# Strassen–Winograd feed-forward: the second group's first product moved ahead of the first group's summed products, and the down projection begun with its three products without sums

## The chip, the cores and the metric

The kernel runs on one core of a Trainium2 chip. TensorE (PE) multiplies, VectorE (DVE) and ScalarE (ACT) do the work on elements, GpSimd (POOL) has little to do here, SyncE (SP) issues the loads of weights. The metric is the device time of one execution in microseconds (us); of several runs the median counts.

## The reference, cut to what matters

The network is two blocks one after the other on 256 tokens of width 1024, all in float32. The parts that the change touches are its feed-forwards, six in all:

```python
def conv_ffn(h, norm_g, w_up, conv_w, conv_b, w_down):          # twice, in the first block
    u = dwconv_centred(rmsnorm(h, norm_g) @ w_up, conv_w, conv_b)
    return (jax.nn.gelu(u[..., :D_FF]) * u[..., D_FF:]) @ w_down

def swiglu(h, wg, wu, wd):
    return (jax.nn.silu(h @ wg) * (h @ wu)) @ wd

def half_ffn(h, g, shift, scale, gate, wg, wu, wd):              # four times, in the second block
    return h + 0.5 * gate * swiglu(modulate(rms_norm(h, g), shift, scale), wg, wu, wd)
```

`D_FF` is 2816, which is 22 tiles of 128 (`FT`); 1024 is 8 tiles (`KT`). The first three half feed-forwards work on 512 columns (256 tokens of context and 256 of the latent), the last one and the two convolutional ones on 256.

## The kernel before

**Seven products in place of eight.** The feed-forward is done in groups of two output tiles by two halves of the columns. A group is a 2 by 2 block product, and class `Fast` computes it with seven products in place of eight, as Winograd's form of Strassen's method does. Call them P1 to P7, as `q` in the code. P1 and P2 use the weights and the activations as they are. P3 uses the weights' last sum and plain activations. P4 uses plain weights and the activations' last sum. P5, P6 and P7 use a sum of weights and a sum of activations each. One product is 4 tiles deep in the up projection (gate and up together) and 11 deep in the down projection, and each depth step of float32 shows as two records in the profile, so that a product has 8 or 22 of them. A product is 256 columns wide ("wide") in the first three half feed-forwards and 128 ("narrow") in the last one and in the convolutional ones.

**The groups.** `i` counts them: 0 to 21 are the gate/up groups, one for each tile of the hidden layer, and 22 to 25 are the four groups of the down projection, each of two output tiles. The convolutional feed-forwards compute their up projection in another way and use `Fast` for groups 22 to 25 alone. P5(22) stands below for the fifth product of group 22.

**The order on TensorE** is that in which `tensor_fast` writes it. It goes through the groups and in each through `PRODUCTS`, which is P1, P5, P6, P7, P3, P2, P4; in group 0 of a half feed-forward it is `FIRST_PRODUCTS`, which is P1, P3, P2, P5, P6, P7, P4, since the activation sums are not there yet. TensorE takes its instructions in that order, and each wait stands in front of a product. P1 and P2 add up in `bank_a`, P7 and P4 in `bank_c`. For that reason P2 waits until P1 has been copied out (by ScalarE, line 1537, in group 0 line 1523), and P4 waits until P7 has been read (by VectorE, line 1617). P1 of the next group waits for the silu that reads `bank_a` (line 1545), or, in the down projection, for the addition to x that reads it (line 1589 or, with the gate of a half feed-forward, 1591, called by line 1645).

**VectorE** takes its instructions in the order of `vector_fast`. For each group it adds u = P1 + P6 (1610), reads P7 (1617), reads P5 twice (1619, 1621) and P3 (1624). In the down projection it then adds two of the four results to x (1639, 1641), makes two weight sums of the next group (1643), adds the third result, which stands in `bank_a`, to x (1645), makes a third weight sum, reads P4 (1653), adds the fourth result and makes the fourth sum. A weight sum (line 1570) is 128 x 512 in the up projection and 128 x 1408 in the down one. The activation sums are made once for a projection, in `vector_activation_sums`: T1 (line 1575) for P5, T2 for P6, one in place for P7, T4 for P4. In the down projection they are as large as half of the hidden layer.

**The loads** of down weights go into a ring of four slots. The load of a later group waits for P2 and P4 of the group whose slots it takes.

Of the kernel before, what the change touches and what calls it, by code (L numbers as in the profile page):

```python
# [11 lines left out]
ACT = mybir.ActivationFunctionType  # L12
# [15 lines left out]
FT = D_FF // 128  # L28
# [70 lines left out]
def build(nc, ins, out):  # L99
# [1253 lines left out]
    bank_a, bank_b, bank_c, bank_d, bank_e = acc[0], acc[1], acc[2], acc[3], aux[0]  # L1353
# [54 lines left out]
    class Fast:  # L1408
# [3 lines left out]
        def __init__(self, t0, up=True, hid_at=None, rows=None):  # L1412
# [11 lines left out]
            for i in range(self.start, n):  # L1424
                for q in FIRST_PRODUCTS if i == 0 else PRODUCTS:
                    if (i < FT and q == 4 and i % 2) or (i >= FT and q in PRODUCTS[-2:]):
                        self.done[i, q] = (acc_full, next(ends))
                    else:
                        self.done[i, q] = (st_p, st_p.reserve(1)(0))
# [39 lines left out]
    def tensor_fast(F, norm_ready=None, following=None):  # L1469
        for i in range(F.start, F.n):  # L1470
            up, j, first = i < FT, i - F.start, i == F.start
            for blk in F.blocks_of(i):
                te.wait_ge(weights_in[blk.slot].sem, blk.arrived_at)
# [6 lines left out]
            banks = {1: bank_a, 2: bank_a, 3: bank_e, 4: bank_c, 5: bank_d, 6: bank_b, 7: bank_c}  # L1480
            for q in FIRST_PRODUCTS if i == 0 else PRODUCTS:
                if q in SUM_FOR:
                    te.wait_ge(st_s.sem, F.s(4 * j + (SUMS if i else FIRST_SUMS)[SUM_FOR[q]]))
                if q in TERM_FOR and i in (F.start, FT):
                    te.wait_ge(st_t.sem, F.t((4 if j and i == FT else 0) + TERM_FOR[q]))
                if q == 1 and first and not up:
                    for b in range(4):
                        te.wait_ge(acc_free[b].sem, F.banks[b])
                elif q == 1 and not first and i <= FT:
                    te.wait_ge(st_g1.sem, F.g1(i - 1))  # L1490
                elif q == 1 and not first:
                    te.wait_ge(st_x.sem, F.x(4 * (i - FT - 1) + 2))
                elif q == 2:
                    te.wait_ge(st_u.sem, F.u(j))
                elif q == 3 and not first:
                    te.wait_ge(st_c12.sem, F.c12(j - 1))
                elif q == 4:
                    te.wait_ge(st_v.sem, F.v(j))
                elif q == 5 and not first:
                    te.wait_ge(st_d.sem, F.d(j - 1))  # L1500
                elif q == 6 and not first:
                    te.wait_ge(st_b.sem, F.b(j - 1))
                elif q == 7 and not first:
                    te.wait_ge(st_c21.sem, F.c21(j - 1))
                lhs, rhs = operands[q]
                for k in range(kt):
                    if i == 0 and q in (1, 3, 2):
                        sig, value = norm_ready(k if q == 1 else 4 + k, 1 if q == 3 else 0)
                        te.wait_ge(sig.sem, value)
                    elif i == FT and q == 1:  # L1510
                        sig, value = (st_hid, F.hid(2 * k + 1)) if F.up else F.hid_at(k)
                        te.wait_ge(sig.sem, value)
                    ins_ = mm(banks[q][:, 0:F.H], lhs[:, k, :], rhs[:, k, :], k == 0 and q not in (2, 4), k == kt - 1)
                F.done[i, q][0].on(ins_)
        if following is not None:
            tensor_norm(following)
        else:
            te.wait_ge(st_x.sem, F.x(14))
            te.wait_ge(st_c21.sem, F.c21(F.n - 1 - F.start))

    def scalar_first_copy(F):
        ac.wait_ge(F.done[0, 1][0].sem, F.done[0, 1][1])
        st_u.on(ac.copy(F.temps[0][:, 0, :], bank_a[:, 0:F.H]))

    def scalar_fast(F, following=None):
        u, v, g1, g2 = F.temps
        for i in range(F.start, F.n):
# [3 lines left out]
            if i:  # L1531
                ac.wait_ge(F.done[i, 1][0].sem, F.done[i, 1][1])
                if j >= 2 and i - 2 < FT:
                    ac.wait_ge(st_hid.sem, F.hid(2 * (i - 2) + 1))
                elif j >= 2:
                    ac.wait_ge(st_x.sem, F.x(4 * (i - 2 - FT) + 3))
                st_u.on(ac.copy(u[:, s, :], bank_a[:, 0:F.H]))  # L1537
# [3 lines left out]
            if i < FT:  # L1541
# [3 lines left out]
                st_g1.on(ac.activation(g1[:, s, :], bank_a[:, 0:F.H], ACT.Silu))  # L1545
# [38 lines left out]
    def vector_fast(F, gate_of=None, following=None):  # L1584
# [8 lines left out]
        for i in range(F.start, F.n):  # L1593
# [43 lines left out]
            if down >= 0:  # L1637
# [7 lines left out]
                add_back(2 * down, 0, bank_a[:, 0:F.H])  # L1645
# [1412 lines left out]
```

## Time and profile before

| | |
|---|---|
| median of 3 runs | 2951.45 us (2949.49 to 2951.77) |
| the profiled execution | 2949.65 us, of it 2948.3 us of span |
| granted TensorE clock, mean | 0.997 of full speed |
| PE busy | 2858.4 us, 97% of the span |
| DVE busy | 1702.3 us, 58% |
| ACT busy | 602.3 us, 20% |
| DMA | 376.15 MB, mean 128 GB/s |

PE is busy in nearly the whole span. What is left to find are short gaps between its products. The timelines further down show them: each line is a run of instructions of one engine on one tile, and the brackets at its end tell how long the engine stood idle before it and which instruction released it.

### The profile page before, as it was taken

How to read it: one execution, taken by the hardware profiler on the slowest of the kernel's cores; microseconds unless marked ns; L12 is line 12 of the kernel's file. 1: busy time of each engine (PE TensorE's matmuls, PEld its weight loads, DVE VectorE, ACT ScalarE, POOL GpSimd, SP SyncE). 2: the span in 40 equal slices, each digit the busy share in tenths (PEclk: the TensorE clock that was granted, in tenths of full speed). 3: DMA queues.
4: the chain of work that ended last, by engine and by line, in shares of the span. 5: the costliest groups of instructions: out<-in, count | busy, mean ns of one | idle time of the engine just before them, and what ended most of it. 6: DMA issues, size and time to landing. Idle time of an engine off the chain costs nothing.

```text
span 2948.3 us, 41101 instructions
## 1 busy us (share of the span) xinstructions
PE 2858.4 (97%) x16754; PEld 2351.4 (80%) x16754; DVE 1702.3 (58%) x3407; ACT 602.3 (20%) x1371; POOL 37.6 (1%) x60
## 2 busy tenths in 40 slices
PE   8988999999999999999999999999999999999999
PEld 7777888977889888888644468888888888766999
DVE  4386467444566477773225457775377773235775
ACT  1264221134221310000124420000110100234110
POOL 0000000020000000000000000000000000000000
PEclk9999999999999999999999999999999999999999
DMA  6400475562665545423213034432444423322444
GB/s 239 139 2 3 167 237 149 189 170 95 218 227 135 186 145 171 152 70 113 75 31 114 3 127 162 160 115 75 133 142 157 152 85 92 106 79 86 144 145 113
DMA packets 349215, 376.15 MB, mean 128 GB/s; under 512 B 7299, under 2 KB 302612, under 8 KB 348260
## 3 DMA queue, kind: packets, MB, share of 16 engines
q1 hardware_dynamic: 323748, 285.68, 31.6%
q10 hardware_dynamic: 23072, 82.52, 7.6%
q0 software_dynamic: 2208, 5.31, 0.9%
q8 instruction: 135, 2.21, 0.3%
q14 instruction: 52, 0.43, 0.0%
HBM read 372.44 MB, written 1.05 MB: 127 GB/s over the span
## 4 chain that ended last, share of the span: by engine, by line
PE 91%; DVE 4%; ACT 3%; issue 1%; DMA 0%; SPq 0%; DVEq 0%; ACTq 0%
PE acc L134 76%; PE aux L134 14%; ACT sb_xn L302 1%; PE aux L2558 1%; DVE sb_work L1570 1%; DVE sb_big L1400 0%; DMA sb_work<-c_decay 0%; DVE sb_work L1400 0%; PE aux L2020 0%; ACT sb_rstd L290 0%; DMA sb_x<-xT 0%; DVE sb_xn L278 0%; DVE sb_work L2769 0%; ACT sb_rstd L292 0%; ACT sb_work L2666 0%
## 5 line engine op out<-in xcount | busy, mean ns | idle before, releaser
L134 PE MATMUL acc<-sb_xn,weights 128*128 128x256 f32 (+3 forms) x5184 | 1218.9, 389 | 17.9 <-DVE sb_xn L278 8.2
L134 PEld LDWEIGHTS acc<-sb_xn,weights 128*128 128x128 f32 (+1 forms) x5184 | 942.0, 190 | 246.8 <-issue 122.9
L134 PE MATMUL acc<-sb_work 128*128 128x256 f32 (+1 forms) x1944 | 374.1, 346 | 2.9 <-DVE sb_work L1575 2.9
L134 PEld LDWEIGHTS acc<-sb_work 128*128 128x128 f32 x1944 | 323.6, 191 | 38.2 <-issue 4.0
L134 PE MATMUL acc<-sb_work,weights 128*128 128x256 f32 (+2 forms) x1508 | 322.2, 361 | 5.8 <-DVE sb_work L1617 3.5
L134 PE MATMUL acc<-sb_big,weights 128*128 128x256 f32 (+1 forms) x1776 | 315.5, 334 | 4.1 <-issue 3.9
L134 PEld LDWEIGHTS acc<-sb_big,weights 128*128 128x128 f32 x1776 | 279.7, 192 | 31.0 <-issue 5.5
L134 PEld LDWEIGHTS acc<-sb_work,weights 128*128 128x128 f32 x1508 | 254.1, 191 | 54.3 <-issue 26.4
L1537 ACT COPY sb_work<-acc 128x256 f32<-128x256 f32 (+1 forms) x108 | 36.7, 340 | 683.9 <-PE acc L134 683.9
L1610 DVE TENSOR_TENSOR sb_work<-sb_work,acc 128x256 f32<-128x256 f32 (+1 forms) x112 | 42.6, 381 | 218.0 <-PE acc L134 218.0
L1543 ACT ACTIVATE sb_work<-sb_work 128x256 f32<-128x256 f32 (+1 forms) x88 | 34.4, 391 | 562.3 <-DVE sb_work L1624 562.3
L134 PE MATMUL aux<-sb_xn,sb_work 128*128 128x256 f32 (+1 forms) x704 | 148.6, 354 | 0.1
L1570 DVE TENSOR_TENSOR sb_work<-weights 128x512 f32<-128x512 f32 (+1 forms) x112 | 99.7, 890 | 75.0 <-PE acc L134 73.6
L134 PEld LDWEIGHTS aux<-sb_xn,sb_work 128*128 128x128 f32 x704 | 122.0, 190 | 14.2 <-ACT sb_xn L302 0.3
L1400 DVE SCALAR_TENSOR_TENSOR sb_work<-sb_work 128x1024 f32<-128x1024 f32 x100 | 122.1, 1221 | 1.4
L1400 DVE SCALAR_TENSOR_TENSOR sb_big<-sb_work 128x1024 f32<-128x1024 f32 x100 | 121.9, 1219 | 0.0
L134 PE MATMUL aux<-sb_big,sb_work 128*128 128x128 f32 (+3 forms) x592 | 109.3, 339 | 0.0
L1624 DVE TENSOR_TENSOR sb_work<-sb_work,aux 128x256 f32<-128x256 f32 (+1 forms) x112 | 42.5, 379 | 103.5 <-PE aux L134 103.5
L1570 DVE TENSOR_TENSOR weights<-weights 128x512 f32<-128x512 f32 (+1 forms) x112 | 99.6, 890 | 2.9
L1570 DVE TENSOR_TENSOR sb_work<-sb_work,weights 128x512 f32<-128x512 f32 (+1 forms) x112 | 99.3, 886 | 3.0 <-DVE sb_work L1570 0.5
L1570 DVE TENSOR_TENSOR sb_work<-weights,sb_work 128x512 f32<-128x512 f32 (+1 forms) x112 | 99.2, 885 | 0.7
L134 PEld LDWEIGHTS aux<-sb_big,sb_work 128*128 128x128 f32 (+1 forms) x592 | 88.7, 185 | 10.9 <-issue 2.8
(352 smaller groups left out, 2664.5 us busy)
## 6 DMA issues: line engine op xcount, KB each, us to landing
weights<-ffn_w_up SPq DMA_DIRECT2D x88, 1024.0 KB, 9.1
weights<-ffn_w_down SPq DMA_DIRECT2D x48, 1408.0 KB, 7.1
sb_work<-w_mod_rows ACTq DMA_DIRECT2D x100, 512.0 KB, 6.0
weights<-ffn_w_gate SPq DMA_DIRECT2D x44, 1024.0 KB, 5.5
sb_big<-w_mod_rows ACTq DMA_DIRECT2D x44, 512.0 KB, 4.8
weights<-mix_w_in SPq DMA_DIRECT2D x5, 2048.0 KB, 12.6
weights<-ple_w_gate SPq DMA_DIRECT2D x4, 2048.0 KB, 7.9
weights<-na_w_qkv SPq DMA_DIRECT2D x8, 1024.0 KB, 7.9
```

Source lines behind the costliest of these rows:

```text
L134: return te.matmul(o, lhsT, rhs, start=start, stop=stop, skip_group_check=True)
L302: shifted.on(ac.activation(y, y, ACT.Identity, bias=N.shift(k, h)))
L1400: rows_done.on(ve.scalar_tensor_tensor(row if s else R.junk, row, 1.0, R.silu_cond[:, s, :], ALU.mult, ALU.mult, accum_out=mod[:, R.first ...
L1537: st_u.on(ac.copy(u[:, s, :], bank_a[:, 0:F.H]))
L1543: st_g2.on(ac.activation(g2[:, s, :], g2[:, s, :], ACT.Silu))
L1570: st_s.on(ve.tensor_tensor(to, one, other, op))
L1610: st_b.on(ve.tensor_tensor(u, u, bank_b[:, 0:F.H], ALU.add))
L1624: st_c12.on(ve.tensor_tensor(g2, g2, bank_e[:, 0:F.H], ALU.add))
L2558: ins_ = te.transpose(aux[u % 3][:, c:c + 128], mx_e[:, u % 4, W * i + 128 * kt:W * i + 128 * kt + 128], ident[:])
```

## The change

Three things are changed in `Fast`, all in the order of TensorE and in the bank of one group.

1. In the half feed-forwards P1 of group 1 is moved from behind P4(0) to in front of P5(0). It goes to a bank of its own: `bank_a` of group 1 is `aux[2]`, and of all other groups `acc[0]` as before. Its wait for the silu of group 0 is left out.
2. In the first down group (22) of all six feed-forwards the order is P1, P3, P2, P5, P6, P7, P4 in place of P1, P5, P6, P7, P3, P2, P4.
3. P3(22) and P2(22) now wait at each of their depth steps for the hidden tile that they read, as P1(22) did before.

The orders of VectorE, ScalarE, GpSimd and SyncE stay as they are.

```diff
-    PRODUCTS, FIRST_PRODUCTS = (1, 5, 6, 7, 3, 2, 4), (1, 3, 2, 5, 6, 7, 4)
+    PRODUCTS = (1, 5, 6, 7, 3, 2, 4)
+    FIRST_TWO = [(0, 1), (0, 3), (0, 2), (1, 1)] + [(0, q) for q in (5, 6, 7, 4)] + [(1, q) for q in (5, 6, 7, 3, 2, 4)]
...
-    bank_a, bank_b, bank_c, bank_d, bank_e = acc[0], acc[1], acc[2], acc[3], aux[0]
+    bank_b, bank_c, bank_d, bank_e = acc[1], acc[2], acc[3], aux[0]
+
+    def bank_a(i):
+        return aux[2] if i == 1 else acc[0]
...
-            for i in range(self.start, n):
-                for q in FIRST_PRODUCTS if i == 0 else PRODUCTS:
...
+            self.order = [(i, q) for i in range(self.start, n) for q in PRODUCTS]
+            if up:
+                self.order[0:2 * len(PRODUCTS)] = FIRST_TWO
+            at = len(PRODUCTS) * (FT - self.start)
+            self.order[at:at + len(PRODUCTS)] = [(FT, q) for q in (1, 3, 2, 5, 6, 7, 4)]
...
-        for i in range(F.start, F.n):
+        for i, q in F.order:
...
-                elif q == 1 and not first and i <= FT:
-                    te.wait_ge(st_g1.sem, F.g1(i - 1))
-                elif q == 1 and not first:
+            elif q == 1 and not first and i != 1 and i <= FT:
+                te.wait_ge(st_g1.sem, F.g1(i - 1))
+            elif q == 1 and not first and i != 1:
...
-                    elif i == FT and q == 1:
-                        sig, value = (st_hid, F.hid(2 * k + 1)) if F.up else F.hid_at(k)
+                elif i == FT and q in (1, 3, 2):
+                    f = k if q == 1 else FH + k
+                    sig, value = (st_hid, F.hid(2 * f + 1)) if F.up else F.hid_at(f)
```

The place in the up projection is seen on TensorE at the start of the first half feed-forward. Before, the rows from P5(0) to P5(1) (acc3 is the bank of P5, acc1 that of P6, acc2 that of P7 and P4, acc0 that of P1 and P2) are:

```order
L134 MATMUL acc3<-sb_work 128x256 [waits activation_sum_set,weight_sum_set]
L134 MATMUL acc3<-sb_work 128x256 x3
L134 MATMUL acc1<-sb_work 128x256 [waits activation_sum_set,weight_sum_set]
L134 MATMUL acc1<-sb_work 128x256 x3
L134 MATMUL acc2<-sb_xn,weights2 128x256 [waits activation_sum_set,weight_sum_set]
L134 MATMUL acc2<-sb_xn,weights2 128x256 x3
L134 MATMUL acc2<-sb_work,weights2 128x256 [waits seventh_product_read,activation_sum_set]
L134 MATMUL acc2<-sb_work,weights2 128x256 x3
L134 MATMUL acc0<-sb_xn,weights2 128x256 [waits left_gate_set]
L134 MATMUL acc0<-sb_xn,weights2 128x256 x3
L134 MATMUL acc3<-sb_work 128x256 [waits fifth_product_read,weight_sum_set]
```

After the change the same stretch reads:

```order
L134 MATMUL aux2<-sb_xn,weights2 128x256 x4
L134 MATMUL acc3<-sb_work 128x256 [waits activation_sum_set,weight_sum_set]
L134 MATMUL acc3<-sb_work 128x256 x3
L134 MATMUL acc1<-sb_work 128x256 [waits activation_sum_set,weight_sum_set]
L134 MATMUL acc1<-sb_work 128x256 x3
L134 MATMUL acc2<-sb_xn,weights2 128x256 [waits activation_sum_set,weight_sum_set]
L134 MATMUL acc2<-sb_xn,weights2 128x256 x3
L134 MATMUL acc2<-sb_work,weights2 128x256 [waits seventh_product_read,activation_sum_set]
L134 MATMUL acc2<-sb_work,weights2 128x256 x3
L134 MATMUL acc3<-sb_work 128x256 [waits fifth_product_read,weight_sum_set]
```

P1(1) has gone from between P4(0) and P5(1) to the head of the stretch, and P5(1) now follows P4(0) directly.

The place in the down projection is seen on TensorE in group 22 of the first convolutional feed-forward (aux0 is the bank of P3). Before, the rows from P5(22) to P4(22) are:

```order
L134 MATMUL acc3<-sb_xn,sb_work 128x128 [waits activation_sum_set,weight_sum_set]
L134 MATMUL acc3<-sb_xn,sb_work 128x128 x10
L134 MATMUL acc1<-sb_work 128x128 [waits activation_sum_set,weight_sum_set]
L134 MATMUL acc1<-sb_work 128x128 x10
L134 MATMUL acc2<-sb_big,weights2 128x128 [waits activation_sum_set,weight_sum_set]
L134 MATMUL acc2<-sb_big,weights2 128x128 x10
L134 MATMUL aux0<-sb_big,sb_work 128x128 [waits weight_sum_set]
L134 MATMUL aux0<-sb_big,sb_work 128x128 x10
L134 MATMUL acc0<-sb_big,weights1 128x128 [waits first_product_copied]
L134 MATMUL acc0<-sb_big,weights1 128x128 x10
L134 MATMUL acc2<-sb_work,weights2 128x128 [waits seventh_product_read,activation_sum_set]
```

After the change the same stretch, with the beginning of P1(23) as its last row, reads:

```order
L134 MATMUL aux0<-sb_big,sb_work 128x128 [waits hidden_tile_set] x10
L134 MATMUL acc0<-sb_big,weights1 128x128 [waits hidden_tile_set,first_product_copied]
L134 MATMUL acc0<-sb_big,weights1 128x128 [waits hidden_tile_set] x10
L134 MATMUL acc3<-sb_xn,sb_work 128x128 [waits activation_sum_set,weight_sum_set]
L134 MATMUL acc3<-sb_xn,sb_work 128x128 x10
L134 MATMUL acc1<-sb_work 128x128 [waits activation_sum_set,weight_sum_set]
L134 MATMUL acc1<-sb_work 128x128 x10
L134 MATMUL acc2<-sb_big,weights2 128x128 [waits activation_sum_set,weight_sum_set]
L134 MATMUL acc2<-sb_big,weights2 128x128 x10
L134 MATMUL acc2<-sb_work,weights2 128x128 [waits seventh_product_read,activation_sum_set]
L134 MATMUL acc2<-sb_work,weights2 128x128 x10
L134 MATMUL acc0<-sb_big,weights3 128x128 [waits x_half_added,weights_arrived0,weights_arrived3]
```

P3 and P2, which stood between P7(22) and P4(22), have moved in front of P5(22). P4(22) with its wait `seventh_product_read` now follows P7(22) directly, and P1(23) with its wait `x_half_added` comes one product after P7(22) in place of three.

## Rows read from the trace of the kernel before

**Rows 1.** The page, part 4: the chain that ended last, by engine.
```profile
PE 91%; DVE 4%; ACT 3%; issue 1%; DMA 0%; SPq 0%; DVEq 0%; ACTq 0%
```

**Rows 2.** Waits of PE, whole run: us in total, times, longest us.
```profile
PE acc L134 <- DVE sb_xn L1575: 2.5, 2, 2.0
```

**Rows 3.** Timeline, first half feed-forward, groups 0 and 1: start us, us, engine.
```profile
1030.58 1.99 PE L134 MATMUL acc<-sb_xn,weights 128*128 128x256 f32 x8 [0.86 <-ACT sb_work L1523]
...
1033.54 3.69 PE L134 MATMUL acc<-sb_work 128*128 128x256 f32 x16 [0.96 <-DVE sb_work L1575]
...
1039.07 0.42 DVE L1617 TENSOR_TENSOR sb_work<-sb_work,acc 128x256 f32<-128x256 f32 x1 [1.08 <-PE acc L134]
...
1039.63 1.97 PE L134 MATMUL acc<-sb_work,weights 128*128 128x256 f32 x8 [0.67 <-DVE sb_work L1617]
...
1040.40 0.68 DVE L1570 TENSOR_TENSOR sb_work<-weights 128x512 f32<-128x512 f32 x1
...
1043.16 3.62 PE L134 MATMUL acc<-sb_work 128*128 128x256 f32 x16
```

**Rows 4.** Timeline, fourth (narrow) half feed-forward, groups 0 and 1.
```profile
2738.47 1.95 PE L134 MATMUL acc<-sb_work 128*128 128x128 f32 x16
...
2740.26 1.06 PE L134 MATMUL acc<-sb_xn,weights 128*128 128x128 f32 x8
...
2741.42 0.29 DVE L1617 TENSOR_TENSOR sb_work<-sb_work,acc 128x128 f32<-128x128 f32 x1 [0.61 <-PE acc L134]
...
2742.02 0.28 DVE L1624 TENSOR_TENSOR sb_work<-sb_work,aux 128x128 f32<-128x128 f32 x1
...
2745.14 0.28 DVE L1653 TENSOR_TENSOR sb_work<-sb_work,acc 128x128 f32<-128x128 f32 x1
...
2745.64 1.06 PE L134 MATMUL acc<-sb_xn,weights 128*128 128x128 f32 x8
```

**Rows 5.** Timeline, first half feed-forward, group 22, P1 to P1(23).
```profile
1296.76 4.91 PE L134 MATMUL acc<-sb_big,weights 128*128 128x256 f32 x22
...
1301.50 4.91 PE L134 MATMUL acc<-sb_xn,sb_work 128*128 128x256 f32 x22
...
1320.77 0.42 DVE L1624 TENSOR_TENSOR sb_work<-sb_work,aux 128x256 f32<-128x256 f32 x1 [3.67 <-PE aux L134]
...
1325.45 0.48 DVE L1591 SCALAR_TENSOR_TENSOR sb_x<-acc,sb_small,sb_x 128x256 f32<-128x256 f32 x1
...
1329.99 0.38 PE L134 MATMUL acc<-sb_big,weights 128*128 128x256 f32 x1
```

**Rows 6.** Timeline, first convolutional feed-forward, group 22, P1 to P1(23).
```profile
489.06 4.32 PE L134 MATMUL acc<-sb_big,weights 128*128 128x128 f32 x22 [1.95 <-issue]
...
493.80 2.69 PE L134 MATMUL acc<-sb_xn,sb_work 128*128 128x128 f32 x22 [0.42 <-DVE sb_xn L1575]
...
503.97 0.29 DVE L1624 TENSOR_TENSOR sb_work<-sb_work,aux 128x128 f32<-128x128 f32 x1 [1.77 <-PE aux L134]
...
507.97 0.28 DVE L1589 TENSOR_TENSOR sb_x<-acc,sb_x 128x128 f32<-128x128 f32 x1
...
508.62 2.62 PE L134 MATMUL acc<-sb_big,weights 128*128 128x128 f32 x22
```

**Rows 7.** Timeline, second convolutional feed-forward, group 22: P1, P5 and P1(23).
```profile
907.40 2.69 PE L134 MATMUL acc<-sb_big,weights 128*128 128x128 f32 x22 [1.96 <-issue]
...
912.14 4.32 PE L134 MATMUL acc<-sb_xn,sb_work 128*128 128x128 f32 x22 [2.05 <-DVE sb_xn L1575]
...
928.74 2.69 PE L134 MATMUL acc<-sb_big,weights 128*128 128x128 f32 x22
```

**Rows 8.** Timeline, fourth half feed-forward: last addition from bank_a, then P1(23).
```profile
2893.48 0.34 DVE L1591 SCALAR_TENSOR_TENSOR sb_x<-acc,sb_small,sb_x 128x128 f32<-128x128 f32 x1
...
2894.00 2.66 PE L134 MATMUL acc<-sb_big,weights 128*128 128x128 f32 x22
```

**Rows 9.** Windows: stretch, its us, PE, PEld, DVE, ACT, POOL busy, PEclk, DMA share, GB/s.
```profile
490.00:491.00 1.00, 1.00 (x7) 1.00 (x6) 1.00 (x2) 0.00 (x0) 0.00 (x0) 0.50 1.16 342
```

More of the change, by code:

```diff
@@ L1423, in __init__ @@
             self.done = {}
-            for i in range(self.start, n):
-                for q in FIRST_PRODUCTS if i == 0 else PRODUCTS:
[L1426 to L1429, printed above, removed]
+            self.order = [(i, q) for i in range(self.start, n) for q in PRODUCTS]
[3 more added lines that the diff above has]
+            self.order[at:at + len(PRODUCTS)] = [(FT, q) for q in (1, 3, 2, 5, 6, 7, 4)]
+            for i, q in self.order:
+                if (i < FT and q == 4 and i % 2) or (i >= FT and q in PRODUCTS[-2:]):
+                    self.done[i, q] = (acc_full, next(ends))
+                else:
+                    self.done[i, q] = (st_p, st_p.reserve(1)(0))
             m = n - self.start
@@ new lines, in tensor_fast @@
+            banks = {1: bank_a(i), 2: bank_a(i), 3: bank_e, 4: bank_c, 5: bank_d, 6: bank_b, 7: bank_c}
+            if q in SUM_FOR:
+                te.wait_ge(st_s.sem, F.s(4 * j + (SUMS if i else FIRST_SUMS)[SUM_FOR[q]]))
+            if q in TERM_FOR and i in (F.start, FT):
+                te.wait_ge(st_t.sem, F.t((4 if j and i == FT else 0) + TERM_FOR[q]))
+            if q == 1 and first and not up:
+                for b in range(4):
+                    te.wait_ge(acc_free[b].sem, F.banks[b])
+            elif q == 1 and not first and i != 1 and i <= FT:
+                te.wait_ge(st_g1.sem, F.g1(i - 1))
+            elif q == 1 and not first and i != 1:
+                te.wait_ge(st_x.sem, F.x(4 * (i - FT - 1) + 2))
+            elif q == 2:
+                te.wait_ge(st_u.sem, F.u(j))
+            elif q == 3 and not first:
+                te.wait_ge(st_c12.sem, F.c12(j - 1))
+            elif q == 4:
+                te.wait_ge(st_v.sem, F.v(j))
+            elif q == 5 and not first:
+                te.wait_ge(st_d.sem, F.d(j - 1))
+            elif q == 6 and not first:
+                te.wait_ge(st_b.sem, F.b(j - 1))
+            elif q == 7 and not first:
+                te.wait_ge(st_c21.sem, F.c21(j - 1))
@@ new lines, in tensor_fast @@
+            lhs, rhs = operands[q]
+            for k in range(kt):
+                if i == 0 and q in (1, 3, 2):
+                    sig, value = norm_ready(k if q == 1 else 4 + k, 1 if q == 3 else 0)
+                    te.wait_ge(sig.sem, value)
+                elif i == FT and q in (1, 3, 2):
+                    f = k if q == 1 else FH + k
+                    sig, value = (st_hid, F.hid(2 * f + 1)) if F.up else F.hid_at(f)
+                    te.wait_ge(sig.sem, value)
+                ins_ = mm(banks[q][:, 0:F.H], lhs[:, k, :], rhs[:, k, :], k == 0 and q not in (2, 4), k == kt - 1)
@@ L1515, in tensor_fast @@
+            F.done[i, q][0].on(ins_)
         if following is not None:
@@ L1522, in scalar_first_copy @@
         ac.wait_ge(F.done[0, 1][0].sem, F.done[0, 1][1])
-        st_u.on(ac.copy(F.temps[0][:, 0, :], bank_a[:, 0:F.H]))
+        st_u.on(ac.copy(F.temps[0][:, 0, :], bank_a(0)[:, 0:F.H]))
     def scalar_fast(F, following=None):
@@ L1536, in scalar_fast @@
                     ac.wait_ge(st_x.sem, F.x(4 * (i - 2 - FT) + 3))
-                st_u.on(ac.copy(u[:, s, :], bank_a[:, 0:F.H]))
+                st_u.on(ac.copy(u[:, s, :], bank_a(i)[:, 0:F.H]))
             if F.rows and 2 <= i <= ROWS_UNTIL:
@@ L1544, in scalar_fast @@
                 ac.wait_ge(F.done[i, 2][0].sem, F.done[i, 2][1])
-                st_g1.on(ac.activation(g1[:, s, :], bank_a[:, 0:F.H], ACT.Silu))
+                st_g1.on(ac.activation(g1[:, s, :], bank_a(i)[:, 0:F.H], ACT.Silu))
                 if F.rows and i == 0:
@@ L1644, in vector_fast @@
                 ve.wait_ge(F.done[i, 2][0].sem, F.done[i, 2][1])
-                add_back(2 * down, 0, bank_a[:, 0:F.H])
+                add_back(2 * down, 0, bank_a(i)[:, 0:F.H])
                 if late:
```

35 lines of the change are left out of this document (3 added, 32 removed).

## The prediction

> **What bounds the kernel now.** I read the chain of waits first: PE holds 91% of it [rows 1], so that only what PE does or waits for counts. PE's list of waits then tells what the change can take away. Its wait for T1 in the down projection comes to 2.5 us in two places [rows 2]. Its wait for T1 at the start of the up projection is 0.96 us at the first half feed-forward [rows 3]; the second and third, which are as wide, repeat this place to within 0.01 us, and the fourth has none [rows 4]. That is all that the new orders can hide: some 5.5 us, and what a gap does to the clock. Last I read the timelines of PE and DVE around each place where the order changes, to see which waits stood behind cover that now moves. In PE's rows the time from the start of one product to the start of the next is what counts; it comes to 1.73 us for a wide up product (the 16 records at 1043.16 are two of them) and 0.89 for a narrow one (two from 2738.47 to 2740.26) [rows 3, 4], to 4.75 for a wide down product (six from 1301.50 to 1329.99) and 2.47 for a narrow one (six from 493.80 to 508.62) [rows 5, 6]. I call E the moment at which the next product could follow P7 with no wait.
>
> **Part 1, the up projection, wide (three times).** P2(0) starts at 1030.58 and with its 0.08 us of restart would be followed at 1032.38; P5(0) starts at 1033.54 [rows 3]. P1(1) with its 1.73 us now fills that gap of 1.16 us, and P5(0) starts at 1034.11. Two products and P7(0) later E comes 0.49 us later than before. P4(0) still waits for L1617, which begins 0.28 us behind E, lasts 0.42 and is seen by PE 0.14 later (1039.07 to 1039.63 [rows 3]), so it starts at 1040.12. It is now followed by P5(1), not by P1(1): 1043.16 - 1.73 + 0.49 = 1041.92, which is **1.24 us earlier**. Is something late instead? P5(1) needs the first weight sum of group 1, which DVE begins 1.33 us behind L1617 and which lasts 0.68 [rows 3]: ready at 1041.7, 0.2 us before it is wanted. The copy of P1(1), now out of aux2, comes behind the silus as before and has a product and a half to spare. So 3 x -1.24 = **-3.7**.
>
> **Part 1, narrow (once).** Here P5(0) did not wait [rows 4]. P1(1) in front of it just makes P5(0), P7(0) and L1617 0.89 us later, and with L1617 all that DVE does up to L1653, which reads P4(0): it ran at 2745.14 and now at 2746.03. P7(1) waits for it, and 0.28 + 0.14 us later is 2746.45. By PE's own order P7(1) would be at 2745.64 as before [rows 4]. P1(1) was the cover of DVE's four weight sums, and it is gone: **+0.8**, and since DVE's row of work stays 0.89 late to P4(1), I take **+0.85**.
>
> **Part 2, the gap at P5(22).** P1, P3, P2 now run while DVE makes T1, and P3's weight sum and the last hidden tile are there before P1(22) ends. The gain is the gap: none in the three wide ones, where P5(22) follows P1(22) at 4.74 us [rows 5] (the whole run has only the two waits of rows 2), none in the fourth half feed-forward (under 0.1), 0.58 us in the first convolutional one (489.06 + 4.32 - 0.16 to 493.80 [rows 6]; 0.16 is how far the modelled end of a product overlaps the next) and 2.27 in the second (907.40 + 2.47 to 912.14 [rows 7]).
>
> **Part 2, what P3 and P2 covered.** They stood between P7(22) and P4(22) and hid two things. (a) P4(22) waits for L1617: E + 0.28 + 0.42 + 0.14 = E + 0.84 wide (as at P4(0) [rows 3]), E + 0.27 + 0.29 + 0.14 = E + 0.70 narrow [rows 4]. (b) P1(23) waits for the addition that reads bank_a, and in DVE's order two weight sums of 1408 columns and two other additions stand ahead of it, all behind the reads of P7, P5 and P3. From L1617 to L1624 it is 0.60 narrow [rows 4], 1.00 wide (0.33 for each of three). From L1624 to that addition it is 4.00 narrow (503.97 to 507.97 [rows 6]) and 4.68 wide (1320.77 to 1325.45 [rows 5]); the wide one may have stood for the end of P2 for some of it, and I take 4.6. Then the addition, 0.48 wide and 0.28 narrow, and 0.14. So P1(23) can start at E + 0.28 + 1.00 + 4.6 + 0.48 + 0.14 = **E + 6.5 wide** and at E + 0.27 + 0.60 + 4.00 + 0.28 + 0.14 = **E + 5.29 narrow**, while P4(22) would be through at E + 5.6 and E + 3.2. Before, this work lay under P2 and P4: narrow, PE reached P1(23) just when it was free.
>
> Place by place, P1(23) after against before:
> - wide, three times: E = 1296.76 + 6 x 4.75 = 1325.26, P1(23) at 1331.76 against 1329.99 [rows 5]: +1.77, in all **+5.3**;
> - first convolutional: E = 493.22 + 5 x 2.47 = 505.57, P1(23) at 510.86 against 508.62 [rows 6]: **+2.2**;
> - fourth half feed-forward: before, P4 was followed at 2894.00 with no wait, so E = 2894.00 - 2.47; its additions are about 0.06 us longer each (0.34 against 0.28 [rows 6, 8]), which makes E + 5.47: **+3.0**;
> - second convolutional: E = 907.40 + 6 x 2.47 = 922.22, P1(23) at 927.51 against 928.74 [rows 7]: -1.2 if its slow stretch goes, **+0.5** if an equal one stays.
>
> **The clock.** In two places 22 records took 4.32 us in place of 2.69 [rows 6, 7], 1.63 us more. The granted clock there is 0.50 [rows 9], that is 1.2 GHz; before each, PE had stood idle for 1.95 and 2.05 us. A third idle time of 1.96 us, at 907.40, was followed by no such stretch [rows 7]. After the change five idle times of about 2 us stand in the kernel: the two before P1(22) of the convolutional feed-forwards, and a new one before P1(23) in each of the three narrow down projections (E + 3.17 to E + 5.29, 2.1 us). The wide ones leave 0.9 us, too short by these rows. Two of three had the drop before; about half of five is 2 to 3 after. I take between none and one stretch more than in the profiled run: +0 to +1.6.
>
> The section "Why this matters for your kernels" of the Trainium skill's page "TensorE: Matmul & The Clock Gate" lets only longer idle gaps than these lower the clock; by it no gap here, old or new, costs a stretch. The rows speak against it (1.95 us idle, then 0.50). By it the sum would stay at +8.15 with no upper case.
>
> **The sum**, against the profiled execution's own 2949.65 us: -3.7 + 0.85 + 5.3 + 2.2 + 3.0 + 0.5 = **+8.15**, with as many slow stretches as it had. That gives 2957.8, and one stretch more 2959.4. The median of the runs is 1.8 us above the profiled one, as much as one such stretch, and from it the two are 2959.6 and 2961.2. I predict **2960**.
>
> The other edits at nothing: the 22 more waits for hidden tiles in P3(22) and P2(22) stand for tiles that are there (P1(22) has such waits and its 22 records take 2.69 us [rows 7], as those of P5(22) without them [rows 6]). Down weights of group 24 may be issued two to three products earlier, since P2(22) ends earlier; nobody waited for them.
>
> **Rivals.**
> - *The DVE row is not late* (the other side: not slower). If the additions that free bank_a were done by the time P4(22) is through, only (a) is paid: wide +0.84 each, first convolutional +0.1, fourth half +0.7, second convolutional -1.6 with its stretch kept. Sum: -3.7 + 0.85 + 2.5 + 0.1 + 0.7 - 1.6 = -1.2, or -2.8 without the stretch: 2947 to 2950. It decides from DVE needing under 5.6 us wide and 3.2 us narrow from E to the addition's end; the rows say 6.4 and 5.2. Chance 0.07.
> - *The clock falls in all the new idle times*: +8.15 and two to three stretches, 2961 to 2965.5. Chance 0.12.
> - *The clock is kept*: the second convolutional's stretch is gone and the new idle times bring none, +4.9 to +6.5: 2954.5 to 2958. Chance 0.14.
> - *The up projection's gain is given back* where DVE, late with its sums in groups 1 and 20, bounds it anyway: +8.15 + 3.7, 2961.5 to 2963.5. Against it, DVE's late work waits for PE's products and so moves with them. Chance 0.05.
> - The forecast, 2957.5 to 2961.5: 0.62.
>
> **The numbers.** The range takes in the kept clock and nearly all of the drops: 2955 to 2965. A measurement here can tell 0.2%, 5.9 us, from no change, so slower begins at 2957.4. Slower holds the forecast without its low edge (0.57), the two dear rivals (0.17) and a part of the kept clock (0.04): 0.78. Same holds the rest of those and most of the first rival: 0.19. Faster: 0.03.
>
> **What would show it.** Right: in PE's waits, L1575 gone for sb_xn and for the wide up starts; new waits of 0.5 to 0.7 us for the read of P7 at six P4(22); new waits at six P1(23) for the addition to x, 0.7 to 0.9 us wide and 2.0 to 2.2 narrow; a new wait of some 0.8 us at P7(1) of the fourth half feed-forward. P1(22) to P1(23) of the first half feed-forward grows from 33.2 to 35.0 us. Wrong: if P1(23) follows P4(22) with no gap, or if gaps of 2 us at P1(23) show 0.50 clock nowhere or everywhere.

## The result, and the profile after

The changed kernel took 2964.99 us, median of 4 runs (2963.09 to 2967.69), beside 2950.59 us of the kernel before in 4 runs. The ratio is 1.0045 with a 95% interval of 1.0033 to 1.0057: **slower by about 13 us** (the medians lie 14.4 us apart). It was timed twice more, beside many more runs of the kernel before, and came to 1.0034 (1.0022 to 1.0046) and 1.0037 (1.0023 to 1.0050), which is 10 to 11 us. Over 68 runs in the batches of the experiments the kernel before spreads from 2949.1 to 2958.2 us; the four runs of it in the first comparison are all at the low end, and that comparison shows some 3 us more than the others.

I read PE's list of waits first. These are lines of it that changed, in the profiled execution of the changed kernel. Lines past the diff have moved by ten: 1627 was 1617 (the read of P7), 1663 was 1653 (the read of P4), 1580 was 1570 (the weight sums), and 1599 and 1601 are the additions to x. The numbers are us in total, times, longest us.

```profile
PE acc L134 <- DVE sb_work L1627: 7.2, 11, 1.0
...
PE acc L134 <- DVE sb_work L1663: 5.1, 5, 1.6
PE acc L134 <- DVE sb_x L1599: 4.1, 2, 2.2
PE acc L134 <- DVE sb_x L1601: 3.8, 4, 2.1
```

The waits for T1 are gone, all five, those of [rows 2] among them. In their place PE waits for the read of P7 in 11 places where it was 5, and in six places for an addition to x, which PE did not wait for before. Those six are the P1(23) of the six feed-forwards.

The timeline of PE at the first down group of the first half feed-forward answers to [rows 5]. In the brackets stand the idle time before the line and what ended it.

```profile
1306.48 4.91 PE L134 MATMUL acc<-sb_big,weights 128*128 128x256 f32 x22
1311.23 4.91 PE L134 MATMUL aux<-sb_big,sb_work 128*128 128x256 f32 x22
...
1330.22 4.91 PE L134 MATMUL acc<-sb_big,weights 128*128 128x256 f32 x22
1335.81 4.99 PE L134 MATMUL acc<-sb_work,weights 128*128 128x256 f32 x22 [0.67 <-DVE sb_work L1627]
1341.38 4.99 PE L134 MATMUL acc<-sb_big,weights 128*128 128x256 f32 x22 [0.58 <-DVE sb_x L1601]
```

P1(22) starts at 1306.48 and P1(23) at 1341.38: 34.90 us where it was 33.23. What held P1(23) is seen in DVE's timeline of the same stretch:

```profile
1335.24 0.42 DVE L1627 TENSOR_TENSOR sb_work<-sb_work,acc 128x256 f32<-128x256 f32 x1 [4.33 <-PE acc L134]
...
1336.24 0.42 DVE L1634 TENSOR_TENSOR sb_work<-sb_work,aux 128x256 f32<-128x256 f32 x1
1336.69 0.88 DVE L1601 SCALAR_TENSOR_TENSOR sb_x<-sb_work,sb_small,sb_x 128x256 f32<-128x256 f32 x2
1337.49 1.62 DVE L1580 TENSOR_TENSOR sb_work<-weights 128x1408 f32<-128x1408 f32 x1
1339.21 1.62 DVE L1580 TENSOR_TENSOR sb_work<-sb_work,weights 128x1408 f32<-128x1408 f32 x1
1340.76 0.48 DVE L1601 SCALAR_TENSOR_TENSOR sb_x<-acc,sb_small,sb_x 128x256 f32<-128x256 f32 x1
```

DVE stood idle for 4.33 us and could then do nothing of this earlier, since all of it is queued behind the read of P7. The two weight sums of the next group (1580) take 3.3 us of the way to the addition that frees the bank.

The narrow places of the same execution, in the first and second convolutional feed-forward and the fourth half feed-forward, answer to [rows 6 to 8]:

```profile
511.29 2.69 PE L134 MATMUL acc<-sb_work,weights 128*128 128x128 f32 x22 [0.54 <-DVE sb_work L1627]
515.87 2.69 PE L134 MATMUL acc<-sb_big,weights 128*128 128x128 f32 x22 [1.89 <-DVE sb_x L1599]
...
938.12 4.23 PE L134 MATMUL acc<-sb_big,weights 128*128 128x128 f32 x22 [2.24 <-DVE sb_x L1599]
...
2910.39 4.32 PE L134 MATMUL acc<-sb_big,weights 128*128 128x128 f32 x22 [2.07 <-DVE sb_x L1601]
```

Two of the three new idle times are followed by 22 records in 4.23 and 4.32 us in place of 2.69. The windows of the profile give the granted clock inside the last one (columns as in [rows 9]):

```profile
2911.00:2912.00 1.00, 1.00 (x6) 1.00 (x6) 0.97 (x2) 0.00 (x0) 0.00 (x0) 0.50 1.15 346
```

At the start of the first half feed-forward, in answer to [rows 3], the gap before P5(0) is filled:

```profile
1041.52 1.99 PE L134 MATMUL acc<-sb_xn,weights 128*128 128x256 f32 x8 [0.86 <-ACT sb_work L1533]
1043.35 1.89 PE L134 MATMUL aux<-sb_xn,weights 128*128 128x256 f32 x8
1045.07 3.62 PE L134 MATMUL acc<-sb_work 128*128 128x256 f32 x16
...
1051.09 1.97 PE L134 MATMUL acc<-sb_work,weights 128*128 128x256 f32 x8 [0.68 <-DVE sb_work L1627]
1052.89 3.62 PE L134 MATMUL acc<-sb_work 128*128 128x256 f32 x16
```

At the narrow start, in answer to [rows 4], P7(1) waits for the read of P4(0):

```profile
2756.34 2.05 PE L134 MATMUL acc<-sb_work 128*128 128x128 f32 x16
2758.95 1.13 PE L134 MATMUL acc<-sb_xn,weights 128*128 128x128 f32 x8 [0.55 <-DVE sb_work L1663]
```

### The profile page after: what moved, and what is told of

It reads as the page before. It is cut to its first block, busy times and chain, and to the rows that moved or that the text cites. A ratio compares the mean times of both kernels' runs of the same rounds, so it can differ in the third digit from the quotient of the medians.

```text
span 2966.4 us, 41109 instructions
## 1 busy us (share of the span) xinstructions
PE 2870.4 (97%) x16754; PEld 2359.7 (80%) x16754; DVE 1700.7 (57%) x3407; ACT 601.6 (20%) x1371; POOL 37.6 (1%) x60
## 4 chain that ended last, share of the span: by engine, by line
PE 91%; DVE 5%; ACT 2%; issue 1%; DMA 0%; SPq 0%; DVEq 0%; ACTq 0%
PE acc L134 75%; PE aux L134 15%; DVE sb_work L1580 1%; ACT sb_xn L302 1%; PE aux L2568 1%; DMA sb_work<-c_decay 0%; DVE sb_work L1405 0%; PE aux L2030 0%; DVE sb_big L1405 0%; ACT sb_rstd L290 0%; DMA sb_x<-xT 0%; DVE sb_work L2779 0%; DVE sb_xn L278 0%; ACT sb_rstd L292 0%; ACT sb_work L2676 0%
## 5 line engine op out<-in xcount | busy, mean ns | idle before, releaser
L134 PE MATMUL acc<-sb_xn,weights 128*128 128x256 f32 (+2 forms) x5120 | 1209.0, 390 | 18.4 <-DVE sb_xn L278 8.2
L134 PEld LDWEIGHTS acc<-sb_xn,weights 128*128 128x128 f32 x5120 | 933.6, 191 | 247.1 <-issue 122.9
L1736 DVE SCALAR_TENSOR_TENSOR sb_work<-acc,sb_cols,sb_work 128x255 f32<-128x255 f32 x88 | 42.4, 482 | 88.6 <-ACT sb_work L1723 88.5
```

The lines of the kernel that those rows point to most:

```text
L134: return te.matmul(o, lhsT, rhs, start=start, stop=stop, skip_group_check=True)
L1736: v_step.on(ve.scalar_tensor_tensor(u[:, 1:L], ps[:, 0:L - 1], cols("ffn_cw", 1, 132 * F.i + t), u[:, 1:L], ALU.mult, ALU.add))
```

## Where the time went, place by place

I cut each profiled execution at the starts of PE's products into 21 stretches. Places of the same kind agree to 0.02 us between executions of the same order, so that one profile of each is enough. All times are us, from the first product named to the second; the up start is P1(0) to P5(1), the rest of the up projection P5(1) to P1(22).

| stretch | before | after | difference |
|---|---|---|---|
| wide up start, three times | 17.13 | 15.93 | -1.20 each |
| wide, rest of the up projection | 253.60 | 253.59 | none |
| narrow up projection, P1(0) to P1(22) | 142.34 | 143.23 | +0.89 |
| wide, P1(22) to P1(23), three times | 33.23 | 34.90 | +1.67 each |
| fourth half, P1(22) to P1(23) | 17.27 | 20.28 | +3.01 |
| first convolutional, P1(22) to P1(23) | 19.56, in three profiles with a slow P1(22) | 20.10, or 21.73 with a slow stretch | +0.54 or +2.17 |
| second convolutional, P1(22) to P1(23) | 19.69, or 21.34 with a slow stretch behind P5(22) | 20.47, or 22.08 with a slow stretch | +0.8 without any; +0.74 in the first two profiles, with one in both |
| after P1(23), three narrow ones | no slow stretch | 1.6 more behind some | 0 to +1.6 each |

Without any slow stretch these make -3.6 + 0.9 + 5.0 + 3.0 + 0.5 + 0.8 = **+6.6**. Each slow stretch in the changed down projections adds 1.6.

One line of the comparison is not the change's. The stretch from the start of the kernel to the first P1(22) took 489.06 us in the profile of before and 495.77 in that of after; no instruction in it differs. In later profiles of both orders it lies between 488.9 and 492.7. The windows of the changed kernel's profile (columns as in [rows 9]) show what fills the 6.7 us: the slow clock, in three places that the profile of before passes at 1.00.

```profile
40.00:44.00 4.00, 4.00 (x13) 3.21 (x12) 0.50 (x2) 0.00 (x0) 0.00 (x0) 0.57 1.06 384
129.00:132.00 3.00, 3.00 (x5) 1.33 (x4) 0.61 (x2) 0.59 (x1) 0.00 (x0) 0.50 1.05 342
173.00:180.00 7.00, 6.28 (x97) 6.19 (x98) 3.20 (x6) 2.42 (x6) 0.00 (x0) 0.53 0.00 0
```

What is missing from full clock there is 4 x 0.43 + 3 x 0.50 + 7 x 0.47 = 6.5 us. The third profile of the changed kernel has 1.00 in all three windows and reaches its first P1(22) at 489.05.

## The experiments

My theory was that the two new waits of the down order, the idle times they leave and the clock that falls behind some of them make the loss. The rivals were that the file or its build costs something of its own, that part 1 has a hidden price, and that the clock falls by chance. Each kernel was timed beside the kernel before on its chip. One batch held both parts undone, each part alone and the new idle times filled; a second held the changed kernel again, the addition ahead of the sums and the two versions that keep the gains; a third held the changed kernel a third time and the last two filled ones.

### Both parts undone

```diff
-        return aux[2] if i == 1 else acc[0]
+        return acc[0]
...
-                self.order[0:2 * len(PRODUCTS)] = FIRST_TWO
-            at = len(PRODUCTS) * (FT - self.start)
-            self.order[at:at + len(PRODUCTS)] = [(FT, q) for q in (1, 3, 2, 5, 6, 7, 4)]
+                self.order[0:len(PRODUCTS)] = [(0, q) for q in (1, 3, 2, 5, 6, 7, 4)]
...
-            elif q == 1 and not first and i != 1 and i <= FT:
+            elif q == 1 and not first and i <= FT:
...
-            elif q == 1 and not first and i != 1:
+            elif q == 1 and not first:
...
-                elif i == FT and q in (1, 3, 2):
+                elif i == FT and q == 1:
```

> The changed kernel with both orders, the bank and the waits put back as they were before; the same instructions on every engine as the kernel before, from a file of which other lines differ. My theory (the orders and the slow stretches behind the new idle times account for all of the 14.4 us, between runs the number of slow stretches differs by chance): the time of the kernel before, within 1.5 us. Rival (some 5 us of the difference come from something else in the file or its build): 3 to 7 us above the kernel before.

Measured: 0.9997 (0.9988 to 1.0005) of the kernel before. By this interval nothing else in the file costs more than 1.5 us. Its profile brought something more. Here is PE at the second convolutional group 22:

```profile
912.12 4.00 PE L134 MATMUL acc<-sb_big,weights 128*128 128x128 f32 x22 [1.95 <-issue]
916.86 2.69 PE L134 MATMUL acc<-sb_xn,sb_work 128*128 128x128 f32 x22 [0.74 <-DVE sb_xn L1583]
```

In the old order P5(22) starts 4.74 us behind P1(22), because T1 is there then. P1(22) ran at the slow clock for most of its 4.00 us, and that cost nothing: the wait for T1 took it in. With a fast P1(22), as in [rows 7], the wait is longer and P5(22) starts 4.74 us behind P1(22) all the same.

### The down part alone

```diff
-        return aux[2] if i == 1 else acc[0]
+        return acc[0]
...
-                self.order[0:2 * len(PRODUCTS)] = FIRST_TWO
+                self.order[0:len(PRODUCTS)] = [(0, q) for q in (1, 3, 2, 5, 6, 7, 4)]
...
-            elif q == 1 and not first and i != 1 and i <= FT:
+            elif q == 1 and not first and i <= FT:
...
-            elif q == 1 and not first and i != 1:
+            elif q == 1 and not first:
```

> The down projection's new order alone; the up projection as before. By the timelines of the changed kernel the order alone costs 1.67 us in each wide group 22, 0.5 + 0.7 + 3.0 us in the narrow ones, 9.3 us together, and up to 1.6 us for each slow stretch behind a new idle time: theory 9.3 to 14 us above the kernel before. Rival (the down order costs just what the timelines of one place show, the rest sits elsewhere): 9 to 9.5 us, and no slow stretches that the kernel before has not.

Measured: 1.0034 (1.0022 to 1.0046), 10 us slower. Its stretches from P1(22) to P1(23) are 34.90 wide, 21.73, 20.47 and 20.28 narrow, as in the changed kernel. Of its five idle times of about 2 us only one was followed by the slow clock in the profile, the one before P1(22) of the first convolutional feed-forward. The whole loss is in this part. How much of it the clock adds is not told by this run: 10 us fits the 9.3 of the order alone as well as 9.3 and a stretch more.

### The up part alone

```diff
-            at = len(PRODUCTS) * (FT - self.start)
-            self.order[at:at + len(PRODUCTS)] = [(FT, q) for q in (1, 3, 2, 5, 6, 7, 4)]
...
-                elif i == FT and q in (1, 3, 2):
+                elif i == FT and q == 1:
```

> The up projection's part alone; the down projection as before. Theory: -1.20 us in each of three wide starts, +0.85 in the narrow one, so 2.7 us below the kernel before (plus or minus one slow stretch of 1.6). Rival (moving P1(1) or its bank costs something that the timelines of its place do not show): at or above the kernel before, by 0 to 3 us.

Measured: 0.9991 (0.9982 to 0.9999), 2.7 us faster, which is the theory's number (3 x 1.20 - 0.89 = 2.7). The rival, no gain or a loss, lies just outside the interval, and its profile has the stretches of the changed kernel again: 15.93 at the first wide start and 253.59 behind it. Moving P1(1) to a bank of its own shows no cost beyond its place.

### VectorE's addition ahead of the weight sums

This takes away one of the two new waits and leaves TensorE's order alone.

```diff
                 if late:
-                    vector_weight_sums(F, i + 1, (0, 1))
+                    vector_weight_sums(F, i + 1, () if i == FT else (0, 1))
                 ve.wait_ge(F.done[i, 2][0].sem, F.done[i, 2][1])
                 add_back(2 * down, 0, bank_a(i)[:, 0:F.H])
                 if late:
-                    vector_weight_sums(F, i + 1, (2,))
+                    vector_weight_sums(F, i + 1, (0, 1, 2) if i == FT else (2,))
```

> The changed kernel, with VectorE adding the third result of group 22 (the one in bank_a) to x before the two weight sums of group 23 and not behind them. Theory (the new wait at P1(23) is that row of sums): the wait at P1(23) is gone, P1(22) to P1(23) is 34.07 us wide against 34.90, and 18.0 (19.6 with a slow stretch) in the narrow ones against 20.1 to 22.1; no slow stretch behind P1(23); in all 9 to 12 us below the changed kernel, and 0 to 2 us below the kernel before. Rival (the additions, or P4's own end, hold P1(23) back, and the sums then hold back P5(23)): less than 3 us below the changed kernel, with new waits at P5(23) or P6(23).

Measured: 0.9994 (0.9985 to 1.0003) of the kernel before; the changed kernel in the same batch had 1.0034, so the one wait was worth 1.0034 - 0.9994 = 0.40%, 12 us, at the upper end of the theory. The stretches make 9.0 us of it without the clock, and the slow stretches behind P1(23) that can no longer come some 1.6 more. PE's timeline in the first half feed-forward:

```profile
1322.76 4.99 PE L134 MATMUL acc<-sb_work,weights 128*128 128x256 f32 x22 [0.67 <-DVE sb_work L1627]
1327.58 4.91 PE L134 MATMUL acc<-sb_big,weights 128*128 128x256 f32 x22
1332.33 4.91 PE L134 MATMUL acc<-sb_xn,sb_work 128*128 128x256 f32 x22
```

The wait for P7's read in front of P4(22) is still there, that of P1(23) is gone, and P5(23) follows with no wait for its sum. From P1(22) to P1(23) it is 34.15 us wide, 18.05 in the first convolutional one and 18.04 in the fourth half feed-forward. So the wait before P4(22) costs 0.9 wide (34.15 - 33.24), and the row of sums in front of the addition 0.75 wide and 2.1 to 2.4 narrow.

### The idle times filled

Does the clock fall because TensorE stood idle? The first of these kernels fills the new idle times before P1(23) with 8 products of ones, which are 16 records of 0.12 us on a bank that nobody reads. The second repeats it, the third also fills the 1.95 us before P1(22) of the convolutional feed-forwards.

```diff
+            if q == 1 and i == FT + 1 and F.H == 128:
+                tensor_idle(8)
```

> The changed kernel with 8 products of ones (16 records, some 1.9 us) on TensorE between P4(22) and P1(23) of the three narrow down projections, where it stood idle for 1.9 to 2.2 us. Theory (idle times of about 2 us bring the clock to 0.50 in part of the cases): P1(23) starts where it did, no slow stretch follows any of the three, and the time is 1.6 to 3.3 us below the changed kernel's, 2961.5 to 2963.5. Rival (the clock falls by chance, not from these idle times): slow stretches behind P1(23) as often as without, and the changed kernel's time, 2964 to 2966.

> The changed kernel with the three new idle times before P1(23) filled with products of ones, a second time, beside the changed kernel on the same chip. Theory: no slow stretch behind any of the three P1(23), one third of 3 x 1.6 us saved on average, 0.5 to 3 us below after_third. Rival: slow stretches there as without the filling, same time.

```diff
+            if q == 1 and i == FT and not F.up:
+                tensor_idle(8)
```

> The changed kernel with all five idle times filled: the three before P1(23) and the two of 1.95 us before P1(22) of the convolutional feed-forwards. Theory: no 0.50 clock anywhere from P1(22) to P1(24) of the six down projections; first convolutional group 22 at 20.1 us, second at 20.5; 2 to 4 us below after_third. Rival: slow stretches there as without the filling, same time.

The changed kernel itself ran again in the second and the third batch, as their measure:

> The changed kernel once more, beside the others of this batch. The kernel before spread over 2949.2 to 2957.9 in 28 runs of the last batch, and the changed one over 2963.1 to 2967.7 in 4. Theory (order 11 us where the first down group's slow stretch is there in both, and one or two more slow stretches behind new idle times): 12 to 15 us above the kernel before. Rival (the first comparison was 5 us too large by the stretch before the first feed-forward, which no edit touches): 9 to 11 us.

> The changed kernel a third time, as the partner of the two filled ones. Theory: 9 to 12 us above the kernel before; of its five idle times of about 2 us in the down projections (two before P1(22), three before P1(23)) some two or three are followed by 0.50 clock. So far 14 of 28 such idle times were, over all profiles. Rival (the clock falls at random): fewer than one in five.

Measured, against the kernel before: the changed kernel 1.0034 and 1.0037 (1.0023 to 1.0050); with the new idle times filled 1.0026 (1.0017 to 1.0035) and 1.0025 (1.0014 to 1.0036); with all five filled 1.0017 (1.0008 to 1.0026). The intervals overlap from one step to the next, so that the times alone do not show that filling helps; in the third batch the changed kernel and the one with all five filled are 0.20% apart, 6 us by ratio, more than the 2 to 4 expected. With all five filled no slow stretch is left in these places, and 1.0017 is 5.0 us where the stretches of the order alone make +6.6. For the clock the profiles tell more than the times. In the third kernel the first convolutional group 22 reads:

```profile
486.77 1.95 PE L134 MATMUL aux<-sb_ones 128*128 128x128 f32 x16
488.88 2.69 PE L134 MATMUL acc<-sb_big,weights 128*128 128x128 f32 x22 [0.17 <-issue]
...
506.93 1.95 PE L134 MATMUL aux<-sb_ones 128*128 128x128 f32 x16
```

P1(23) starts where it did without the filling (20.11 us behind P1(22)), and nothing is slow. Here is the count over all profiles of this study, with the two kernels that are described next:

| idle time of 1.89 to 2.26 us | slow stretch behind it |
|---|---|
| before P1(22), first convolutional | 8 of 11 |
| before P1(22), second convolutional | 5 of 11 |
| before P5(22), as in [rows 7] | 1 of 1 |
| before P1(23), new (first, second convolutional, fourth half) | 4 of 12 (0, 1 and 3 of 4) |
| any of these places, filled | 0 of 13 |

So the idle times bring the slow clock, in 18 of 35 cases, and filling them prevents it. Which of them it hits differs from one execution to the next. The 0.58 us at the wide P1(23) were never followed by it: the granted clock is 1.00 around all three in the seven profiles that have them (21 cases). Where between 0.58 and 1.89 us it begins these places do not show, but somewhat shorter idle times elsewhere in the kernel brought it too: in the profile of before PE stood idle for 1.68 us until 751.57, and from 752.50 to 753.50 the granted clock is 0.50.

### A version that keeps the gains

P1(1) is moved only where P5(0) waited. In group 22 P3 alone goes ahead, which covers T1, and P2 stays between P7 and P4, where it covers the read of P7. VectorE adds from bank_a after the first weight sum.

```diff
-                self.order[0:2 * len(PRODUCTS)] = FIRST_TWO
+                self.order[0:2 * len(PRODUCTS)] = FIRST_TWO if t0 == 0 else [(0, q) for q in (1, 3, 2, 5, 6, 7, 4)] + [(1, q) for q in PRODUCTS]
...
-            self.order[at:at + len(PRODUCTS)] = [(FT, q) for q in (1, 3, 2, 5, 6, 7, 4)]
+            self.order[at:at + len(PRODUCTS)] = [(FT, q) for q in (1, 3, 5, 6, 7, 2, 4)]
...
-                elif i == FT and q in (1, 3, 2):
+                elif i == FT and q in (1, 3):
...
-                    vector_weight_sums(F, i + 1, (0, 1))
+                    vector_weight_sums(F, i + 1, (0,) if i == FT else (0, 1))
...
-                    vector_weight_sums(F, i + 1, (2,))
+                    vector_weight_sums(F, i + 1, (1, 2) if i == FT else (2,))
```

> A version that keeps the gains: P1(1) in front of P5(0) in the wide half feed-forwards only; group 22 in the order P1, P3, P5, P6, P7, P2, P4, so that P3 alone covers the making of T1 and P2 covers the read of P7; VectorE adds the result of bank_a after the first weight sum of group 23. Theory: wide starts -1.2 each, wide group 22 as before (33.24), first convolutional 18.9 to 19.0 against 19.56 with its slow stretch, second 17.3 against 19.7, fourth half 17.2 against 17.27; in all 6 to 8 us below the kernel before, some 2945 to 2947. Rival (what P3 or P2 covers is not enough in the narrow places): 3 to 5 us below, with waits of 0.5 us or more left at P4(22) or P1(23).

Measured: 2947.11 us, 0.9976 (0.9967 to 0.9985), **7 us faster than the kernel before**. Its first convolutional group 22 has no idle time from P1(22) on:

```profile
489.03 2.69 PE L134 MATMUL acc<-sb_big,weights 128*128 128x128 f32 x22 [1.95 <-issue]
491.56 2.62 PE L134 MATMUL aux<-sb_big,sb_work 128*128 128x128 f32 x22
494.02 2.62 PE L134 MATMUL acc<-sb_xn,sb_work 128*128 128x128 f32 x22
496.47 2.62 PE L134 MATMUL acc<-sb_work 128*128 128x128 f32 x22
498.93 5.08 PE L134 MATMUL acc<-sb_big,weights 128*128 128x128 f32 x44
503.84 2.62 PE L134 MATMUL acc<-sb_work,weights 128*128 128x128 f32 x22
506.30 2.62 PE L134 MATMUL acc<-sb_big,weights 128*128 128x128 f32 x22
```

From P1(22) to P1(23) it is 17.27 in all three narrow places and 33.24 in the wide ones. The line of 44 records is P7 and P2, now neighbours. Against before the stretches make 3 x 1.20 + (19.56 - 17.27) + (19.69 - 17.27) = 8.3 us less, and a slow P1(22), where it comes, costs 1.6 of that, since P3 follows at once as in the changed kernel; this profile has none.

The same with the filling before P1(22) of the convolutional feed-forwards:

> The last version with 8 products of ones in front of P1(22) of the two convolutional feed-forwards, where TensorE stood idle for 1.95 us before. Theory (the idle time brings the slow stretch): no 0.50 clock in P1(22) to P1(23) of either, 17.3 us in both, 1.6 to 2 us below the last version. Rival (it makes no difference to the clock): a slow stretch of 1.6 us still there in the first convolutional group 22, and the time of the last version within 0.5 us.

Measured: 2943.58 us, 0.9969 (0.9958 to 0.9981), **9 us faster than the kernel before**, with 17.27 in both convolutional places and no slow clock there. That it is faster than the last one, by ratio 2 us, lies inside the intervals. The entry's idle time was not followed by a slow stretch in the profile of the last one, so the two profiles don't tell them apart either: what the filling gains here is not shown.

## Why the prediction was right, and where it was off

The direction and the mechanism were right. The time is not as good as it looks: 2964.99 lies inside the range of 2955 to 2965 by 0.01 us, 5 us above the forecast of 2960 and outside the 2957.5 to 2961.5 that had the chance of 0.62. It lies in the range of the second rival, that the clock falls in all the new idle times, but the profile shows that in two of three, and the rest came from places that the change does not touch. So the range held by luck. What holds without it is the difference to the kernel before in the two later batches, 10 and 11 us (6.5 to 14.8 by the intervals), for the +8.15 to +9.75 of the sum. Step by step:

- **Part 1, wide**: -1.24 each was said, -1.20 measured. The first weight sum of group 1 was in time, as worked out.
- **Part 1, narrow**: +0.85 said, +0.89 measured, by the mechanism named: P7(1) waits for the read of P4(0). Its idle time shows as 0.55, not as the 0.8 of the signs; the start moved as worked out.
- **Wait (a), the read of P7 before P4(22)**: idle 0.5 to 0.7 was said; it is 0.54 narrow and 0.67 wide, in six places.
- **Wait (b), the addition before P1(23)**: 34.90 against 33.23 wide is +1.67 for +1.77 said. From L1634 to the addition it is 4.52 us (1336.24 to 1340.76), not 4.6. The idle time there is 0.58 wide, below the 0.7 to 0.9 of the signs. The fourth half feed-forward has +3.01 for +3.0, the first convolutional one, in later profiles with a slow P1(22) as in that of before, +2.17 (21.73 - 19.56) for +2.2. In the second convolutional one the sum has +0.5, its own terms make -1.23 + 1.63 = +0.4, and measured is +0.74 with a slow stretch in both. The idle time is 2.24 there, not 2.1, because the second weight sum begins 0.46 us late, as it did before the change.
- **The first rival**, that DVE's row is not late, fell by these rows. What it would have taken is seen in the kernel with the addition ahead of the sums: 1.8 us below the kernel before by ratio, between its -1.2 and -2.8, though the interval (-4.4 to +0.9) is wider than the two.
- **The gain given back**: it was not. The rest of the up projection takes 253.6 us before and after.
- **The clock**: this is the term that was too small, and its account was incomplete. I counted as many slow stretches as in the profile of before, or one more, at 1.6 us each, and charged both kernels for those behind P1(22). But in the old order a slow P1(22) cost nothing, since P5(22) waited for T1 to the same moment; the kernel with both parts undone shows it at 912.12. In the new order P3 follows at once, and a slow stretch there is paid in full: 19.56 became 20.10 without and 21.73 with one, where I had put +2.2 and called it the order's. With the shares of the table, 8/11 + 5/11 stretches at the entries and 3 x 4/12 behind the new idle times are 2.2 stretches, 3.6 us: 6.6 + 3.6 = 10.2 us, near the 10 and 11 of the two later batches. Their intervals begin at 6.5 and 6.8 us and so hardly speak against the bare 6.6, and the sum charges the kernel before nothing for a slow P5(22), which cost it 1.65 us (21.34 - 19.69) in its first profile. So the size of this term is an estimate; that it is there is shown by the places.
- **What is left**: the first comparison's 13.3 us are 3 more than that. The profiled execution of the changed kernel lost 6.7 us at the slow clock ahead of the first P1(22), where no instruction differs, and two other profiles of the same kernel lost at most 1.6 there against before. The kernel before was at the low end of its spread besides. The three other runs of the first comparison have no profile, but their mean granted clock is 0.995, where that of the profiled one is 0.994 and that of the kernel before 0.997. That the place of these stretches is chance is argued from this, not shown by a run of its own.
- **The rule from the Trainium skill's page "TensorE: Matmul & The Clock Gate"** ("Why this matters for your kernels") asks for no idle gaps above about 3 us. That is not strict enough here: idle times of 1.9 to 2.3 us, shorter than those it warns of, were followed by 0.50 clock in 18 of 35 cases, and in none of 13 where they were filled.

## What to carry to other kernels

A product that seems free to move may be the cover of something behind it: before moving it, ask not only what it covers in its new place but what stood in its shadow in the old one, on every engine that reads the neighbours' results. Here moving one product (P3) was enough to cover the gap (with VectorE's addition behind one weight sum; without that edit it was not run), which is 2.3 and 2.4 us in the two places that had one; moving the second (P2) as well uncovered two reads, and the down part as a whole lost 10 us. And an engine whose row of work starts at one release should do first what frees a buffer, and only then what is wanted a product later. A wait can absorb a slow stretch of the clock: when it is removed, the stretch is paid. And a difference of 0.3% needs more than four runs of each kernel: places that no edit touched moved one execution here by 6.7 us.

## What was not expected of the hardware

- Idle times of about 2 us on TensorE were followed by a stretch at 1.2 GHz (granted clock 0.50) in 18 of 35 cases. It made 22 narrow records take up to 1.63 us longer, which cost as much where the next product followed at once, and nothing where that product waited for T1 anyway. An idle time of 0.58 us was never followed by one, in 21 cases. Eight products of ones in the idle time kept the clock in 13 of 13.
- The kernel with both parts undone spread over 8.8 us in 11 runs on one chip, and the mean granted clock moves with the time: 2949.41 us at 0.998 and 2958.22 us at 0.995. In the profiles the differences lie ahead of the first P1(22) and between the feed-forwards, not in the up projections, which repeat to 0.02 us.
